# One short expert block moved from the front of the list of experts to its end, and one wait taken out

## The reference

```python
def expert_block(args):
    xb, e = args
    return (jax.nn.silu(xb @ lp['w1'][e]) * (xb @ lp['w3'][e])) @ lp['w2'][e]
```

## Time and profile before

| | |
|---|---|
| median of 3 runs | 1350.9 us (1348.52 to 1351.37) |
| the profiled execution | 1351.37 us, its span 1349.6 us |
| granted TensorE clock, mean over the span | 0.971 |
| busy: PE, DVE, ACT, POOL | 1232.8, 418.4, 335.2, 224.5 us |
| PE waits for weights on line 1139 / 1131 / 1188 | 15.9 / 10.8 / 8.7 us |
| weight loads | 96 of 2048 KB, 30.6 us median from issue to landing |
| scatters from 800 us on | 32, 10.3 us median to landing |
| gathers from 800 us on | 28, 11.0 us median to landing |

### The profile page before, as it was taken

How to read it: one execution, slowest core, us unless ns; L and a number is a source line. 1 busy time by engine, 2 the same in 40 slices (tenths; PEclk the granted TensorE clock), 3 DMA queues, 4 the chain that set the end, 5 groups by cost and what they waited for, 6 DMA issues and landing times.

```text
span 1349.6 us, 31532 instructions
## 1 busy us (share of the span) xinstructions
PE 1232.8 (91%) x13258; PEld 874.3 (65%) x13258; DVE 418.4 (31%) x905; ACT 335.2 (25%) x782; POOL 224.5 (17%) x315
## 2 busy tenths in 40 slices
PE   5999999999899999999999889987899899889884
PEld 2554444446566666666666589654799798888862
DVE  2421411015645555554543751111011111111110
ACT  3531121024435545535443100111000000000000
POOL 1220010103312312212211011221011111111111
PEclk9999999999999999999999889999899999999998
DMA  8611111132201201201124889999999999999993
GB/s 333 247 51 39 71 64 40 38 147 82 80 17 64 80 17 65 80 17 58 53 81 175 343 292 366 381 360 393 382 384 369 374 378 368 373 377 376 383 372 89
DMA packets 44668, 278.63 MB, mean 206 GB/s; under 512 B 10056, under 2 KB 15176, under 8 KB 31772
## 3 DMA queue, kind: packets, MB, share of 16 engines
q1 hardware_dynamic: 36656, 254.80, 48.7%
q0 software_dynamic: 6624, 17.84, 5.5%
q10 hardware_dynamic: 1296, 4.72, 0.9%
HBM read 252.58 MB, written 29.83 MB: 209 GB/s over the span
## 4 chain that ended last, share of the span: by engine, by line
PE 65%; DMA 21%; issue 5%; DVE 2%; ACT 2%; POOL 2%; SPq 1%; another core or an unknown queue 0%; ACTq 0%; POOLq 0%; DVEq 0%
DMA arena<-in_w 20%; PE psum L1067 17%; PE psum L1131 8%; PE psum L970 8%; PE psum L1013 5%; PE psum L1188 4%; PE psum L1045 4%; PE psum L1139 3%; PE psum L1025 2%; PE psum L843 2%; PE psum L914 2%; PE psum L1176 2%; PE psum L858 2%; POOL small L1592 1%; PE psum L955 1%
## 5 line engine op out<-in xcount | busy, mean ns | idle before, releaser
L1067 PE MATMUL psum<-arena 128*128 128x512 f32 (+1 forms) x576 | 242.1, 579 | 1.3 <-DMA arena<-in_w_in 1.3
L1131 PE MATMUL psum<-arena 128*64 128x80 f32 (+1 forms) x5632 | 224.3, 241 | 16.3 <-DMA arena<-in_w 10.8
L1131 PEld LDWEIGHTS psum<-arena 128*64 128x64 f32 x5632 | 216.4, 139 | 24.5 <-DMA arena<-in_w 12.3
L1067 PEld LDWEIGHTS psum<-arena 128*128 128x128 f32 x576 | 109.6, 192 | 125.9 <-issue 125.4
L1188 PE MATMUL psum<-arena 128*64 128x96 f32 (+1 forms) x2816 | 116.4, 244 | 20.9 <-issue 12.2
L970 PE MATMUL psum<-arena 128*128 128x512 f32 x288 | 126.9, 593 | 1.8 <-DVE arena L2023 1.0
L1188 PEld LDWEIGHTS psum<-arena 128*64 128x64 f32 x2816 | 112.8, 138 | 23.8 <-issue 14.0
L970 PEld LDWEIGHTS psum<-arena 128*128 128x128 f32 x288 | 53.3, 190 | 63.2 <-issue 61.6
L1533 ACT ACTIVATE arena<-psum,slot_gate 96x1024 f32<-96x1024 f32 x22 | 24.4, 1110 | 280.3 <-PE psum L1198 280.3
L1139 PE MATMUL psum<-arena 128*64 128x256 f32 x640 | 77.6, 400 | 15.9 <-DMA arena<-in_w 15.9
L1461 ACT ACTIVATE arena<-psum 16x128 f32<-16x128 f32 (+4 forms) x172 | 57.6, 398 | 128.4 <-PE psum L1025 128.4
(11 more groups left out here) (248 smaller groups left out, 1305.3 us busy)
## 6 DMA issues: line engine op xcount, KB each, us to landing
arena<-in_w SPq DMA_DIRECT2D x96, 2048.0 KB, 30.6
z_rows<-arena SPq DMA_DIRECT2D x27, 256.0 KB, 2.0
arena<-z_rows SPq DMA_DIRECT2D x9, 768.0 KB, 5.6
arena<-in_w_in SPq DMA_DIRECT2D x3, 2048.0 KB, 21.2
arena<-in_x_rows ACTq DMA_DIRECT2D x9, 512.0 KB, 4.3
arena<-in_xT_rows SPq DMA_DIRECT2D x9, 512.0 KB, 12.4
arena<-in_x_rows SPq DMA_DIRECT2D x9, 512.0 KB, 6.4
out_y<-arena SPq DMA_DIRECT2D x9, 512.0 KB, 2.6
```

The costliest lines, as they stand in the source:

```text
L1067: ins = pe.matmul(o[:, 0:w], xT[n][:, k, :], w_in[:, at_ + k * w:at_ + (k + 1) * w], start=(k == 0), stop=(k == KD - 1))
L1131: ins = pe.matmul(o[c:c + CT, j * EB:j * EB + rows], w[:, k, j * P + c:j * P + c + CT], x[:, k, 0:rows], start=(k == 0), stop=(k == KD - 1))
```

## The change

One position of 64 rows leaves the front: positions 3 to 9 have 64 rows, 10 to 14 have 96, 15 to 28 have 80, and 29, 30, 31 have 64. The ranks follow: position 3 before held rank 24 of the list by falling count, and that expert now stands at position 31; all others of the long blocks and of the tail move one position to the front, and keep their rank's number of rows. The number of positions of each size is the same.

The buffer sets shift with it: positions 0 to 9 rotate over 0, 1, 2; 10 to 28 alternate between 1 and 2; 29 takes set 0, which nothing has used since position 9; 30 takes set 2 and 31 set 1. The loops of all engines start and end one position earlier. Apart from that `hidden_3` loses its wait for `xeT_read`, which `hidden_1` of the same position has already made.

```diff
--- before.py
+++ after.py
@@ -60,10 +60,10 @@
 EL = 80
 ET = 64
 FIRST = 3
-CAPS = [EB] * 3 + [ET] * 8 + [EB] * 5 + [EL] * 14 + [ET] * 2
-SETS = [p % 3 for p in range(11)] + [2 * (p % 2) for p in range(11, 30)] + [1, 0]
+CAPS = [EB] * 3 + [ET] * 7 + [EB] * 5 + [EL] * 14 + [ET] * 3
+SETS = [p % 3 for p in range(10)] + [1 + p % 2 for p in range(10, 29)] + [0, 2, 1]
 EARLY, LATE = CAPS.index(ET), len(CAPS) - CAPS[::-1].index(EL)
-LOOPS = ((12, 16), (16, 30))
+LOOPS = ((11, 15), (15, 29))
 CT = 64
 FT = FF // 2
 MAX_OVER = 27
@@ -796,13 +796,13 @@
 
                 load_ups(sp_, p, SETS[p], before_it(p) + 1, between)
 
-            for p in range(FIRST, 14):
+            for p in range(FIRST, 13):
                 load_turn(p)
-            with sp_.Fori(0, (30 - 14) // 2) as j:
+            with sp_.Fori(0, (29 - 13) // 2) as j:
                 for i in range(2):
-                    p = 2 * j + 14 + i
-                    load_ups(sp_, p, SETS[14 + i], p - 1, lambda: load_down(sp_, p - 1, SETS[13 + i], p - 2))
-            for p in range(30, NE):
+                    p = 2 * j + 13 + i
+                    load_ups(sp_, p, SETS[13 + i], p - 1, lambda: load_down(sp_, p - 1, SETS[12 + i], p - 2))
+            for p in range(29, NE):
                 load_turn(p)
             load_down(sp_, NE - 1, SETS[NE - 1], before_it(NE - 1) + 1)
 
@@ -1151,7 +1151,6 @@
             def hidden_3(w, s, b, arrived, count, rows):
 
                 pe.wait_ge(arrived, count)
-                pe.wait_ge(xeT_read, b + 1)
                 pe.wait_ge(hh_ok, b)
                 ins = up_by_tokens(bank(3), w3s[w], xeT[s]) if rows == ET else up(bank(3), w3s[w], xeT[s], rows)
                 ins.then_inc(h3_full, 1)
@@ -1556,12 +1555,12 @@
 
             act.wait_ge(order_ok, 1)
             silu_tanh(0, EB)
-            for p in range(0, 12):
+            for p in range(0, 11):
                 turn(p)
-            with act.Fori(0, (28 - 12) // 2) as j:
+            with act.Fori(0, (27 - 11) // 2) as j:
                 for i in range(2):
-                    turn(12 + i, j)
-            for p in range(28, NE):
+                    turn(11 + i, j)
+            for p in range(27, NE):
                 turn(p)
             act.wait_ge(over_ok, 1)
             total = act.value_load(over_e[0:1, MAX_OVER:MAX_OVER + 1], min_val=0, max_val=MAX_OVER)
@@ -1731,13 +1730,13 @@
             e = column(3)
             pool.wait_ge(xeT_full, 2)
             gather(1, 3, e, xe_in[1], EB)
-            for p in range(0, 12):
+            for p in range(0, 11):
                 turn(p)
-            for lo, hi in ((12, 16), (16, 28)):
+            for lo, hi in ((11, 15), (15, 27)):
                 with pool.Fori(0, (hi - lo) // 2) as j:
                     for i in range(2):
                         turn(lo + i, j)
-            for p in range(28, NE):
+            for p in range(27, NE):
                 turn(p)
             pool.wait_ge(over_ok, 1)
             total = pool.value_load(over_e[0:1, MAX_OVER:MAX_OVER + 1], min_val=0, max_val=MAX_OVER)
@@ -2318,12 +2317,12 @@
             xeT_take(1, 1, EB)
             hidden(0)
             list_overflow()
-            for p in range(1, 12):
+            for p in range(1, 11):
                 turn(p)
-            with dve.Fori(0, (28 - 12) // 2) as j:
+            with dve.Fori(0, (27 - 11) // 2) as j:
                 for i in range(2):
-                    turn(12 + i, j)
-            for p in range(28, NE):
+                    turn(11 + i, j)
+            for p in range(27, NE):
                 turn(p)
             hT_take(NE - 1)
             total = dve.value_load(over_e[0:1, MAX_OVER:MAX_OVER + 1], min_val=0, max_val=MAX_OVER)
```

## The result

The changed kernel takes 1362.78 us (1360.51 to 1364.67, 4 runs) against 1349.71 us of the kernel before (1347.3 to 1351.37, 4 runs): a ratio of 1.0098, with a 95% interval of 1.0074 to 1.0121. That is 13 us slower, and outside the range that was given.

A forecast was written before the change was run, and what follows sets the result against it. The prediction took the weights' loads to set the pace. All terms were 0 except -0.05 us for the dropped wait, so 1351.4 us became 1351.3, or 1350.8 for the median; the range was 1346.0 to 1355.0.

The forecast's parts named there:

- The bytes: Whole stream of loads: same 96 loads, gathered rows and sum of scattered rows, so its end stays; term 0.
- the shorter front: Short positions at the front: one fewer moves SP's hold from position 13 to 12, with about the same cover; term 0.
- the longer tail: Positions 29 to 31: no load issued later, same instructions after the last w3 lands; term 0 for the order.
- The hold: SP standing still before a w1 load, now at position 12; TensorE's matmuls would end between 935.4 and 941.6 us.
- The wait taken out: TensorE's queue: one semaphore wait fewer a position, only position 31's on the path; -0.05 us, at most -1.6.
- The clock: Tail products: 1.69 us now lost to the lower clock could be gained or grow; bounds -1.7 to +5.6, taken as 0.
- TensorE in the long positions: 96-row and 80-row positions: entered one position sooner with the same work and loads ahead; term 0.
- Being late there only shortens the 28 us queue.: Long positions: TensorE's lateness would only shorten the queue of loads, with 19.9 us of waits to give; term 0.
- the sign of being right: Tail: the last w3 product would begin within 1.5 us of 1325.6.
- a hold run dry: DMA queue during SP's hold: cover gone, shown by a share under 0.97 behind 930 us; bounds 0 and 2.5 us.
- The rivals: Whole kernel: uneven DMA engines 1346.5 us (0.12), TensorE the bound 1344.8 (0.08), clock 1353.6 to 1356.4 (0.15), no change (0.65).
- the clock in the tail: Products of the last w3 and w2: lower clock costs up to 5.6 us, giving 1353.6 to 1356.4 us; chance 0.15.

The follow-up runs named there:

- e5: Changed kernel with 50 instructions of already met waits just before TensorE's wait for the routing tables, where it stands idle: 1347.93 us.
- e9: Changed kernel with hidden_3's wait for xeT_read put back, so the table of positions alone: 1363.02 us.
- e2: Kernel before with 60 instructions of already met waits at the start of TensorE's program: 1371.83 us.
- e4: Changed kernel with 30 instructions of already met waits at the start of TensorE's program: 1362.68 us.
- e6: Kernel before with 34 instructions of already met waits just before TensorE's wait for the routing tables, where it stands idle: 1354.03 us.
- e10: Changed kernel with 38 instructions of already met waits just before TensorE's wait for the routing tables, where it stands idle: 1408.05 us.
- e12: Kernel before with both of TensorE's loops over positions written out: 1368.31 us.
- e3: Kernel before with 256 instructions of already met waits, one whole block, at the start of TensorE's program: 1363.36 us.

## Why the prediction was wrong

- *The bytes, the shorter front, the longer tail.* Right, as far as e5 shows it: with the loop in seven blocks, the same table gives a ratio of 0.9997. The hold ended at 937.5 us, inside the computed 935.4 to 941.6 us.
- *The wait taken out.* Right: nothing (e9).
- *The clock.* The tail lost less than before: its last w3 product took 3.67 us, so the -1.7 us that the prediction had left to chance came. The clock did fall, but in the loop, behind the pauses (0.69 from 1098 to 1120 us).
- *TensorE in the long positions: term 0.* This step failed. It counted the work of a position and the loads ahead of it, and took the instructions themselves as given. The change moves a piece of written-out code from ahead of the loop to behind it, which brings the loop 186 instructions forward, across a block's edge. I had both orders in front of me, and the move stood in them; I did not ask where a jump back lands. Three reloads cost TensorE 10.9, 10.6 and 7.6 us of pauses, 29.1 us together, and the lower clock behind them, where it had 19.9 us to give in the whole stage.
- *"Being late there only shortens the 28 us queue."* This premise of the same term failed too. SP's waits of up to 18.7 us did shorten the queue, from about 28 us to landing down to about 10, but DMA work was lost from the first of them on, and some 16 us of it in all. So the last w3 product began 14.8 us later, where the prediction had named 1.5 us as the sign of being right. The sign that the prediction had set for a hold run dry, a share under 0.97 behind 930 us, came (0.90) with another cause.
- *The rivals.* None of them was it. The one on the slower side, the clock in the tail, had the right sign and the wrong place. No rival and no term stood for the delivery of instructions.

What stays open: why eight blocks are reloaded in only three of the six repeats in the changed kernel (e2, e4 and e9 have three too, with 91 packets in all as the changed kernel has), in one in e6, and in all six in e10. That a reload takes so long because the DMA engines are full of weights is likely and not shown: no version jumps back over so much code while they are idle. That the queue's packets are TensorE's is inferred, from the pauses beside them and from the 44 that e12 adds.

## What to carry to other kernels

Where TensorE runs a loop with a long body, count its instructions and find its place in the 256-instruction blocks before an edit ahead of it is called free; the regular "issue" pauses of the first iteration, 126 to 128 matmuls apart, give the edges. If a change that should do nothing costs a per cent, look at the instruction packets while the loop repeats: here the versions that kept their speed had none but those for the code behind the loop. A few dozen idle instructions ahead of the loop are the test and the cure, and both kernels should be compared with their loops equally placed.

## What the runs showed of the hardware

The 16 KB packets of code come over the same DMA engines as the weights (91 packets, 0.5% of their time, in the changed kernel). With the share at 1.00, a block of a straight run costs TensorE 0.74 to 1.87 us in the first iteration of the kernel before, and up to 2.5 us in e12. A reload is nine packets, and the wait for the loop's head 7.6 to 10.9 us in the changed kernel and up to 12.1 us in e10. A body of 1620 or 1621 instructions is kept when it touches seven blocks, and reloaded in one to six of its six repeats when it touches eight. A met wait at the program's start is not free: from 60 to 256 instructions of them (e2 and e3) the first matmul moved from 13.56 to 34.73 us, 0.11 us for each instruction.
